# Prologue of a two-block transformer kernel on one core: x in four transfers, weight tiles ahead of the small vectors, spare matmuls on TensorE

## The reference, cut to what matters

```python
h = rmsnorm(x, norm_mix_g[0])
u = h @ w_pw1 + b_pw1
a, gate = jnp.split(u, 2, axis=-1)
u = a * jax.nn.sigmoid(gate)
u = lax.conv_general_dilated(u, w_dw[:, None, :], padding=[(30, 0)], feature_group_count=1024, ...) + b_dw
u = jax.nn.silu(layernorm(u, ln_g, ln_b))
x = x + u @ w_pw2 + b_pw2
mem_n = rmsnorm(mem, norm_memsrc_g[0])     # 256 x 1024, keys and values of a cross attention
...
```

## Time and profile before

| | us |
|---|---|
| median of 3 runs | 2828.13 |
| lowest and highest of them | 2827.51, 2828.43 |
| the profiled execution | 2821.69 |
| its span, first to last instruction | 2819.9 |
| TensorE busy | 2696.6 (96%) |
| VectorE busy | 1128.1 (40%) |
| ScalarE busy | 947.2 (34%) |
| GpSimd busy | 1283.2 (46%) |
| mean granted TensorE clock | 0.973 of full |

### The profile page before, as it was taken

How to read it: one execution, slowest core, us unless ns; L and a number is a source line. 1 busy time by engine, 2 the same in 40 slices (tenths; PEclk the granted TensorE clock), 3 DMA queues, 4 the chain that set the end, 5 groups by cost and what they waited for, 6 DMA issues and landing times.

```text
span 2819.9 us, 31496 instructions
## 1 busy us (share of the span) xinstructions
PE 2696.6 (96%) x12392; PEld 2241.9 (80%) x12392; DVE 1128.1 (40%) x1359; ACT 947.2 (34%) x1285; POOL 1283.2 (46%) x620
## 2 busy tenths in 40 slices
PE   7788699999999999999999999999999988999998
PEld 6667488888888888888888888888888877888887
DVE  7999744312234354444211374421214236321213
ACT  4224334322233354343222332322223246332223
POOL 4554434444443356354444444444444437444442
PEclk9899799999999989999999999999999989999999
DMA  4531221332232212322223322333323311322331
GB/s 155 179 142 38 90 90 60 97 98 97 97 98 88 86 42 79 120 75 97 90 95 105 96 93 90 104 98 97 98 92 95 98 55 43 104 90 94 101 98 59
DMA packets 169854, 262.43 MB, mean 93 GB/s; under 512 B 16370, under 2 KB 78250, under 8 KB 168698
## 3 DMA queue, kind: packets, MB, share of 16 engines
q1 hardware_dynamic: 159690, 235.22, 26.0%
q10 hardware_dynamic: 10032, 25.38, 2.7%
HBM read 254.17 MB, written 11.61 MB: 94 GB/s over the span
## 4 chain that ended last, share of the span: by engine, by line
PE 84%; DVE 5%; issue 5%; POOL 2%; ACT 2%; DVEq 1%; DMA 1%; ACTq 0%
PE ps L750 78%; PE ps L907 2%; PE ps L870 2%; POOL prob L664 2%; PE ps L893 2%; DVE conv L1579 1%; DVE pt_lo L1342 1%; ACT pt_hi L1284 1%; DVEq L1575 0%; PE ps L875 0%; PE ps L680 0%; DVE h_lo L1347 0%; DMA xnat<-in_x 0%; ACT w_hi L982 0%; DVE t L1524 0%
## 5 line engine op out<-in xcount | busy, mean ns | idle before, releaser
L630 POOL TENSOR_TENSOR w_lo<-stage,w_hi 128x1024 fp32r<-128x1024 f32 x444 | 1103.2, 2493 | 1318.9 <-ACT w_hi L982 1318.7
L982 ACT ACTIVATE w_hi<-stage 128x1024 fp32r<-128x1024 f32 x444 | 461.8, 1054 | 1126.2 <-PE ps L750 1114.1
L750 PE MATMUL ps<-h_hi,w_hi 128*128 128x512 f32 x1920 | 753.2, 392 | 4.0 <-DVE h_lo L1347 3.2
L750 PE MATMUL ps<-h_lo,w_hi 128*128 128x512 f32 x1920 | 748.5, 390 | 0.0
L750 PE MATMUL ps<-h_hi,w_lo 128*128 128x512 f32 x1920 | 748.3, 390 | 0.0
L750 PEld LDWEIGHTS ps<-h_hi,w_hi 128*128 128x128 f32 x1920 | 361.4, 188 | 81.2 <-issue 5.8
L750 PEld LDWEIGHTS ps<-h_lo,w_hi 128*128 128x128 f32 x1920 | 361.5, 188 | 77.3 <-issue 2.4
L750 PEld LDWEIGHTS ps<-h_hi,w_lo 128*128 128x128 f32 x1920 | 361.3, 188 | 75.4
L750 PE MATMUL ps<-mid_hi,w_hi 128*128 128x512 f32 x992 | 386.8, 390 | 7.2 <-DVE mid_lo L1342 7.2
L750 PE MATMUL ps<-mid_lo,w_hi 128*128 128x512 f32 x992 | 386.6, 390 | 0.0
L750 PE MATMUL ps<-mid_hi,w_lo 128*128 128x512 f32 x992 | 386.6, 390 | 0.0
(11 more groups left out here) (222 smaller groups left out, 2834.0 us busy)
## 6 DMA issues: line engine op xcount, KB each, us to landing
stage<-in_ff_w SPq DMA_DIRECT2D x256, 256.0 KB, 2.9
stage<-in_ffn_w_gate SPq DMA_DIRECT2D x88, 256.0 KB, 2.8
stage<-in_ffn_w_up SPq DMA_DIRECT2D x88, 256.0 KB, 3.0
stage<-in_ffn_w_down SPq DMA_DIRECT2D x88, 256.0 KB, 2.8
stage<-in_conv_pw_w SPq DMA_DIRECT2D x48, 256.0 KB, 3.1
stage<-in_conv_w_in SPq DMA_DIRECT2D x48, 256.0 KB, 3.0
stage<-in_attn_w_qkv SPq DMA_DIRECT2D x48, 256.0 KB, 3.0
stage<-in_mem_wk SPq DMA_DIRECT2D x32, 256.0 KB, 3.2
```

What stands on the lines that cost most here:

```text
L630: pool.tensor_tensor(w_lo[:, slot], stage[:, slot], w_hi[:, slot].bitcast(F32), ALU.subtract).then_inc(tile_lo, 1)
L750: last = pe.matmul(ps[:, base + n, 0:width], lhs, mov, start=k == 0 and m == 0, stop=k == 2 * tiles - 1 and m == 2)
L982: act.activation(w_hi[:, slot], stage[:, slot], ACT.Copy).then_inc(tile_hi, 1)
```

## The change

- ACT issues x as four transfers, each of two chunks' columns (512 KB, rows of 1 KB), with a semaphore each. It issues no vectors.
- SP issues the first vector's rows (norm_mix_g, 16 rows) first, then the four tiles of the first group, and then the other vectors and tables (21 transfers).
- TensorE runs 12 matmuls of the identity with the ones into bank 6 as soon as the constants are there, turns the gain's rows, pair 0, 4 more such matmuls, pair 1, 4 more. Pair 2 is turned ahead of tile 1 of the first group, pair 3 ahead of tile 2, and the vectors and the table product ahead of tile 3 (`turn_rows`).
- VectorE copies the gain's 16 columns, and then takes the pairs one by one, each followed by its h_lo and its squares. The other columns, the table and the pads come in a step `rows` ahead of `mem_rows`.
- ACT makes h_hi and the squares of one pair at a time, and splits tile p + 1 after pair p.

```diff
-PROLOGUE = dict(pe_side=2 + DC, psum_read=4, step=3)
+PROLOGUE = dict(pe_side=1, step=1)
+TAKE_X = dict(pe_side=1, psum_read=1)
+ROWS = dict(pe_side=2, step=3)
+WARM, WARM_BETWEEN = 12, 4
...
     do("prologue", PROLOGUE)
-    do("prep", prep_counts(0, 2), gain("norm_mix_g"), 0, 2, True, x_pairs=2)
-    do("first_tiles", {}, 1, 2)
-    do("prep", prep_counts(2, 2), gain("norm_mix_g"), 2, 2, True, at_once=True)
-    do("first_tiles", {}, 3, 1)
-
+    for p in range(4):
+        do("take_x", TAKE_X, p)
+        do("prep", prep_counts(p, 1), gain("norm_mix_g"), p, 1, True, reuse=p >= 2)
+        do("first_tiles", {}, p + 1, 1 if p < 3 else 0)
+    do("rows", ROWS)
     do("mem_rows", MEM_ROWS)
-    normed("glu", "pw1", "h")
+    normed("glu", "pw1", "h", first_group=True)
...
@@ SP: group, prologue
+            if first_group:
+                for r, (frm, n) in row_loads[1:]:
+                    sp.dma_start(r, frm).then_inc(rows_in, 16)
 
         def prologue():
-
-            for r, (frm, n) in row_loads[HALF:]:
-                sp.dma_start(r, frm).then_inc(rows_in, 16)
+            r, (frm, n) = row_loads[0]
+            sp.dma_start(r, frm).then_inc(gain_in, 16)
...
@@ TensorE: group, prologue
             for j in range(tiles):
+                if first_group and j in (1, 2):
+                    turn_pair(j + 1)
+                if first_group and j == 3:
+                    turn_rows()
...
+        def warm(n):
+
+            for _i in range(n):
+                pe.matmul(ps[:, 6, 0:P], ident[:, :], ones[:, :], start=True, stop=True)
+
+        def turn_pair(p):
+            pe.wait_ge(x_in[p], 16)
+            if p == 3:
+
+                pe.wait_ge(step, 1)
+            for c in (2 * p, 2 * p + 1):
                 for i in range(TB):
                     last = pe.transpose(ps[:, c, i * P:(i + 1) * P], xnat[:, i, c * P:(c + 1) * P], ident[:, :])
-                last.then_inc(pe_side, 1)
-
+            last.then_inc(pe_side, 1)
+
+        def prologue():
             pe.wait_ge(consts, 2)
-            pe.wait_ge(x_in, 16)
-            for c in range(DC // 2):
-                turn_x(c)
-
+            warm(WARM)
+            pe.wait_ge(gain_in, 16)
+            pe.transpose(ps[:, 7, 0:FIRST_ROWS], vrow[0:FIRST_ROWS, 0, :], ident[0:FIRST_ROWS, 0:FIRST_ROWS]).then_inc(pe_side, 1)
+
+        def take_x(p):
+            if p < 2:
+                turn_pair(p)
+                warm(WARM_BETWEEN)
+
+        def turn_rows():
+
+            pe.wait_ge(psum_read, 4)
             pe.wait_ge(rows_in, ROWS_IN)
             for r in range(4):
...
@@ ACT: prologue
-            act.dma_start(xnat[:, :, :], A["x"][0].rearrange("(i p) d -> p i d", p=P)).then_inc(x_in, 16)
-            for r, (frm, n) in row_loads[:HALF]:
-                act.dma_start(r, frm).then_inc(rows_in, 16)
+            for p in range(4):
+                cols = slice(2 * p * P, 2 * (p + 1) * P)
+                act.dma_start(xnat[:, :, cols], A["x"][0][:, cols].rearrange("(i p) d -> p i d", p=P)).then_inc(x_in[p], 16)
...
@@ VectorE: prologue
+            dve.wait_ge(pe_side, 1)
+            dve.tensor_copy(vec[:, 0:FIRST_ROWS], ps[:, 7, 0:FIRST_ROWS]).then_inc(step, 1)
+
+        def take_x(p):
+            dve.wait_ge(pe_side, b.at("pe_side", 1))
+            dve.tensor_copy(x[:, 2 * p:2 * p + 2, :], ps[:, 2 * p:2 * p + 2, :]).then_inc(psum_read, 1)
+
+        def rows_out():
+            dve.wait_ge(pe_side, b.at("pe_side", 1))
+            dve.tensor_copy(vec[:, FIRST_ROWS:], ps[:, 7, FIRST_ROWS:n_rows]).then_inc(step, 1)
+            dve.wait_ge(pe_side, b.at("pe_side", 2))
             dve.wait_ge(rows_in, ROWS_IN)
             dve.tensor_tensor(g_tab[:, :], flat(ps[0:HEADS, 5:7, :], GCOLS), g_log[:, :], ALU.add).then_inc(step, 1)
...
```

More of the change, by code:

```diff
@@ L477, in build_in @@
     keys_out, keys_back = sem("keys_out"), sem("keys_back")
-    rows_in, x_in, mem_in = sem("rows_in"), sem("x_in"), sem("mem_in")
+    rows_in, gain_in, mem_in = sem("rows_in"), sem("gain_in"), sem("mem_in")
+    x_in = [sem(f"x_in{p}") for p in range(4)]
     g_out, skewed, gates_in, negc_out, stored = (sem(n) for n in ("g_out", "skewed", "gates_in", "negc_out", "stored"))
@@ L541, in build_in @@
     row_loads += [(relb[:, :], (A["rel_bias_2"], 0)), (onehot_sb[:, :], (onehot_c, 0)), (g_log[:, :], (logcount_c, 0))]
-    ROWS_IN = 16 * len(row_loads)
-    HALF = len(row_loads) // 2
+    ROWS_IN = 16 * (len(row_loads) - 1)
+    FIRST_ROWS = rows[0][2]
     block = ctx.enter_context(nc.Block())
@@ L578, in _, with group @@
             src_of[f"down2{layer}"] = plain(A["ffn_w_down_2"][layer])
-        def group(kind, src, g, rhs, dst, fresh, tiles, row0=0, **_):
+        def group(kind, src, g, rhs, dst, fresh, tiles, row0=0, first_group=False, **_):
             nonlocal stage_at
@@ L683, in group @@
                   after_turn=False, columns=False, since=0, two_norms=False, early=None,
-                  layer=0, after=None, **_):
+                  layer=0, after=None, first_group=False, **_):
             r_hi, r_lo = operand[rhs]
@@ L762, in group @@
                 pe.wait_ge(step, b.at("step", 1))
-        def prologue():
-            def turn_x(c):
+        def warm(n):
[6 more added lines that the diff above has]
+            for c in (2 * p, 2 * p + 1):
                 for i in range(TB):
                     last = pe.transpose(ps[:, c, i * P:(i + 1) * P], xnat[:, i, c * P:(c + 1) * P], ident[:, :])
-                last.then_inc(pe_side, 1)
+            last.then_inc(pe_side, 1)
+        def prologue():
             pe.wait_ge(consts, 2)
-            pe.wait_ge(x_in, 16)
-            for c in range(DC // 2):
-                turn_x(c)
+            warm(WARM)
[7 more added lines that the diff above has]
+            pe.wait_ge(psum_read, 4)
             pe.wait_ge(rows_in, ROWS_IN)
@@ L783, in prologue @@
             last.then_inc(pe_side, 1)
[L784 to L788, removed]
         def mem_turn(layer):
@@ L963, in output @@
             turn(TB - 1, 1)
-        schedule(b, dict(prologue=prologue, group=group, mem_turn=mem_turn, conv_pe=conv_pe,
+        schedule(b, dict(prologue=prologue, take_x=take_x, group=group, mem_turn=mem_turn, conv_pe=conv_pe,
                          ln_centred=ln_centred, ln_sum=ln_sum, gates=gates, attend=attend, output=output))
@@ L1123, in diagonal_rounds, with prep @@
                 last.then_inc(diag_hi, 1)
-        def prep(gain, first, n, split, squares=True, whole=False, last=False, twice=None, x_pairs=0, at_once=False):
+        def prep(gain, first, n, split, squares=True, whole=False, last=False, twice=None, reuse=False):
             scale_x = last
@@ L1136, in prep @@
                 if not whole:
-                    act.wait_ge(psum_read, b.at("psum_read", m + 1 - n - x_pairs))
+                    act.wait_ge(psum_read, b.at("psum_read", m + 1 - n))
                 if split:
@@ L1143, in prep @@
                 if squares:
-                    if at_once:
-                        act.wait_ge(step, b.at("step", 2 * (m - 1)))
+                    if reuse:
+                        act.wait_ge(step, b.at("step", -2))
                     if m >= 2:
@@ L1482, in prologue @@
             dve.memset(small[:, 41:42], LN_EPS)
[L1483 to L1491, removed]
+            dve.wait_ge(pe_side, 1)
[7 more added lines that the diff above has]
+            dve.wait_ge(pe_side, b.at("pe_side", 2))
             dve.wait_ge(rows_in, ROWS_IN)
             dve.tensor_tensor(g_tab[:, :], flat(ps[0:HEADS, 5:7, :], GCOLS), g_log[:, :], ALU.add).then_inc(step, 1)
-            take_x(2, 8)
-            take_x(3, 10)
             dve.memset(u_hi[:, :, 0:PAD].bitcast(F32), 0.0)
@@ L1543, in prep @@
                 if not whole:
-                    dve.wait_ge(psum_read, b.at("psum_read", m + 1 - n - x_pairs))
+                    dve.wait_ge(psum_read, b.at("psum_read", m + 1 - n))
                 if split:
@@ L1746, in output @@
                 dve.tensor_scalar(xnat[:, i, 0:S], ps[:, 2 * i, :], small[:, 4 + i:5 + i], None, ALU.mult).then_inc(t_ready, 1)
-        schedule(b, dict(prologue=prologue, group=group, mem_turn=mem_turn, prep=prep, prep_all=prep_all,
+        schedule(b, dict(prologue=prologue, take_x=take_x, rows=rows_out, group=group, mem_turn=mem_turn, prep=prep, prep_all=prep_all,
                          mem_rows=mem_rows, conv=conv_taps, conv_pe=conv_pe, ln_centred=ln_centred,
```

## The result

Measured: 2832.1 us, median of 21 runs (2828.61 to 2833.62), beside 2827.29 for the kernel before (2822.65 to 2828.58, 21 runs). The ratio is 1.0018 (95% interval 1.0012 to 1.0025), and the medians are 4.8 us apart. Forecast were 2830.3 and a range of 2825.8 to 2833.3. The runs of the kernel before lie in two bunches: 4 of the 21 took under 2824 us, the others 2826.0 to 2828.6.

The account below looks back on a forecast made before the run. VectorE's convolution taps were taken to bound the stretch behind the first eviction. Sum of squares -0.3 and half clock +2.5 gave +2.2 us, added to the median 2828.13: 2830.3 us, range 2825.8 to 2833.3.

Parts of the forecast that it names:

- the question: Start of the first group's eviction, 47.37 us before: its shift was to move all later work equally; forecast 49.6.
- the sign: Whole kernel: the change was forecast to make it slower, by 2.2 us.
- the mechanism of the second half: Ahead of tile 3: vectors turned behind tile 2 delay mem_rows, TensorE idles; of 7 us won, 0.3 are left.
- The wait ahead of the sum: TensorE ahead of tile 3's sum of squares: idle from 33.0 to 40.3, 7.3 us, until mem is normalised.
- The chain from tile 2 over the vectors to mem: Tile 2 ends at 31.2, vectors turned by 33.0, table and pads by 34.3, then mem_rows 6.02 us: sum at 40.3.
- The loads: x's four transfers beside the weight tiles: pairs land by 4.8, 8.8, 12.9 and 16.9; costed at nothing.
- three hand-offs give 4.05 us: tile 0 starts at 12.65: Pair 0 on VectorE: copy 1.23, h_hi 1.32, h_lo 1.29 and hand-offs; tile 0 starts 7 us earlier than 19.62.
- clock falls twice: Slower rival: the clock also falls in the gap ahead of tile 0, costing 2.8 us more; +5.0 to +5.8, chance 0.08.
- The clock behind the second wait: Tile 3 after TensorE's idle time: half clock costs 2.5 us, bounds nothing and 2.9.
- Nothing in between can absorb it: Behind the first eviction: a microsecond won or lost ahead of it moves the tap work and everything later by a microsecond.
- Collisions of w_lo: GpSimd's w_lo beside VectorE's pair work: 2.2 us each; two of three meet an addition, TensorE held up about 0.5.
- The spare matmuls: TensorE's start: twelve warm the clock, ending between 6.3 and 7.7; four each after pairs 0 and 1 cost nothing.

Follow-up runs that it names:

- e1: Changed kernel with mem_rows moved between pairs 1 and 2, only the store of g_tab left behind the vectors: 2825.9 us, ratio 0.9994.
- e4: Changed kernel without any of its 20 spare matmuls: 2831.7 us, ratio 1.0018 to the kernel before.
- e3: Changed kernel with VectorE's copy of pair 1 ahead of h_lo of pair 0: 2827.1 us, ratio 1.0002 to the kernel before.
- e2: Changed kernel with 20 instead of 4 spare matmuls after pair 1, filling the wait ahead of tile 0: 2829.6 us, ratio 1.0012.
- e5: Changed kernel with 32 more spare matmuls between the turning of the vectors and tile 3: 2829.6 us, ratio 1.0017.
- e8: Changed kernel with x in one 2 MB transfer on ACT's queue instead of four: 2837.7 us, ratio 1.0042.
- e7: Changed kernel with e3's edit, mem's squares behind pair 1, sum not awaiting vectors or mem, earlier root, later g_tab store: 2820.4 us, ratio 0.9980.
- e10: Kernel before with one edit: the first group's sum of squares no longer waits for mem_rows: 2823.8 us, ratio 0.9991.
- e9: e7 without any spare matmuls: 2821.9 us, ratio 0.9987 to the kernel before.

## Why the prediction was right or wrong

**Right:** the question (when does the first eviction start), the sign, and the mechanism of the second half. The wait ahead of the sum, forecast as 7.3 us and ended by mem's scaling, was 7.26, and e1 took it away for 6.2 us of median. The first copy came at 8.55 (forecast 8.6). The chain from tile 2 over the vectors to mem went as worked out: from the end of tile 2 at 35.9 to the sum at 45.0 are 9.1 us (forecast 31.2 to 40.3, also 9.1). From 15.0 on, TensorE waited for nothing until the vectors were turned. The loads were not on the path of pair 0 (turned at 7.42, straight behind the gain), but it was close: tile 0's weights landed at 8.52 and not by 4.8, ACT's split of them ended at 9.6, and pair 0 was copied at 9.8. In e4, where the pair came earlier, they held it up.

**The step that failed** is "three hand-offs give 4.05 us: tile 0 starts at 12.65". I had tile 0 wait for h_lo of pair 0 alone. Its group first waits for `psum_read` less two (now line 696, line 690 of before), since its products go to the four banks out of which pairs 0 and 1 are copied. In the kernel before both copies were long over; with the pairs one by one, pair 1's copy is queued behind h_lo and the addition of pair 0. That put tile 0 at 15.03, and, with e3's edit, at 13.21. And h_lo of pair 0 itself was done at 13.2 and not at 12.65: beside w_lo of tile 0, a collision that I had not priced, it took 1.91 us instead of 1.29. The sum came 4.7 us late: 2.4 by tile 0's start and 2.7 by its half clock, less the 0.5 that I had laid on for VectorE and that TensorE did not wait.

**The rival "clock falls twice"**, given 0.08, is what happened, under the condition that it named, a gap nearer 3 us (3.85). I had the gap at 1.75 from the same faulty step. It forecast +5.0 to +5.8 at the eviction; measured +5.75. The 2.8 us of half clock in tile 0 are right (2.7, and e2 shows 2.8 at the sum by itself), but that the whole fits is luck: the rival knew nothing of the bank that was not free, so that the sum came 1.9 us later than it has it, and it took the clock behind the second wait 1.1 us too dear.

**The clock behind the second wait:** 2.5 was taken, the trace shows 1.4 (8.12 us from the sum to the eviction, 6.77 before and 6.74 in e5). It is not one number: behind the same wait it is 1.4 in e4 too, 1.9 in e3, 2.4 in the changed kernel's second trace, 2.8 in e2 and 2.9 in e8, so that 2.5 was inside what the runs show. The Trainium skill's page "TensorE: Matmul & The Clock Gate", section "HAM oscillation — how this bites in real kernels", said that the next burst would start cold, and both waits show it; the size goes with the moment at which the clock comes back, 2.9 us after the sum began here, 4.0 in e3 and 5.8 in e2.

**"Nothing in between can absorb it"** was right in direction but too simple: behind the eviction the trace lost a further 2.2 us up to 440, and e7 and e10 lost most of what they had gained, so a shift does not travel unchanged. The last tap loop shows the first of it, to be held against the second of the earlier trace rows:

```profile
251.99 52.26 DVE L1602 SCALAR_TENSOR_TENSOR conv<-u_pad,vec,conv 128x512 f32<-128x512 f32 x52
```

It is 6.8 us late, 1.1 more than the eviction; VectorE's km_lo just ahead of it took 2.23 us instead of 1.29. By the medians the whole came to 4.8, less than the two traces differ; that the forecast's +2.2 is nearer to it than the trace's +9.4 is chance. **Collisions of w_lo** I had priced at 2.2 each and laid on additions of pairs 1 and 2, where TensorE had slack; the one that costs is on the first addition, where there is none, and it comes in some runs only (in the changed kernel's second trace, in e1, e4 and e8).

**The spare matmuls**, priced at nothing, cost nothing (e4) and, as the change has them, gave nothing: the clock that they had raised fell again in the 3.85 us behind them.

## What to carry to other kernels

When a start is cut into pieces, list for the first matmul every semaphore that it waits for, banks that it writes among them, and not only its operands; a wait that was always met before the cut can become the last one. And when a step is moved to where an engine has time, look at what is counted behind it: a wait for "all steps so far" carries a chain of 6 us along that the waiting instruction does not need, and to move that chain into an idle stretch (e1) gave back 6.2 us of median, more than the change had cost (4.8). Spare matmuls are worth nothing if the clock falls again ahead of the real ones: tile 0 went at full clock where they left no wait (e2) or 1.79 us (e3), and it was at half clock for 3 us or more where they left 2.32 us or more (e7, the changed kernel, e1). And a gain at one point of a trace is not yet a gain of the whole: follow it to the end.

## What the runs showed of the hardware that was not expected

- The granted clock reads 1.00 from the start of the trace in the kernel before, yet the first 16 transposes were 0.21 us apart, and later ones 0.11. In e9 it reads 1.00 from 0 to 60 us, yet tile 0's first matmuls were 0.43 apart and its last 0.23. So a 1.00 ahead of the first recorded fall does not tell the level: TensorE's pace there was at first that of the lower one (1.2 GHz).
- Whether VectorE's addition takes 0.68 or 2.82 us was decided by 0.02 us in the first trace of the changed kernel: whichever of it and GpSimd's w_lo starts first goes undisturbed, and the other waits for its end (w_lo 2.87 us where it came second, 2.48 where it came first). The Trainium skill's page "SBUF — State Buffer", section "SBUF: two separate sides", describes an exclusive lock held for a whole instruction, for a VectorE operation with two SBUF inputs against a GpSimd operation that reads SBUF; these rows agree, and the copy from PSUM at 13.76, 1.21 us beside w_lo, does too.
- After 2.32 us without work the clock fell (e7), after 1.79 (e3), 1.59 (before) and 1.24 (e1) it did not. The length of the wait alone does not tell it: in the long waits the fall came 1.6 us (e3, second wait) to 3.4 us (changed kernel, second wait) after TensorE's last work.
- Transfers of one queue delay those of the other: with x in one transfer on ACT's queue (e8), tile 0's weights, issued on SP's from 1.19 as in the changed kernel, came at 13.35 instead of 8.52. That is one trace each, and why is not shown.
